# A small gather moved between two experts' products, with router logits by token, halved refills, nine taps on TensorE and x loaded first

## The reference, cut to what matters

```python
# first block, layer 0 (layer 1 has a recurrent mixer in place of conv_mixer)
u = x @ w_in                                     # 1024 -> 2560
a = a_val * sigmoid(a_gate)
a = causal_depthwise_conv(a, a_dw) + a_dw_b      # 31 taps, 512 channels
a = silu(layer_norm(a, a_ln_g, a_ln_b))
bb = b_b * causal_depthwise_conv(b_c * b_x, b_dw)
m = concatenate([a, bb]) @ w_out
x = layer_norm(ALPHA * x + m, ln1_g, ln1_b)
# route
logits = x @ w_router + b_router                 # 16 experts in 4 groups
probs = softmax(logits)                          # best group, then best 2 of its 4
# expert e on the tokens that chose it
y = (silu(xb @ w1[e]) * (xb @ w3[e])) @ w2[e]
x = layer_norm(ALPHA * x + f, ln2_g, ln2_b)
# second block, layer 0: forgetting attention, then conv_ffn; layer 1: dilated attention, then conv_ffn
h = rms_norm(x, mix_norm_g[layer])
log_f = log_sigmoid(h @ w_f + a_b_f)
```

## Time and profile before

| | us |
|---|---|
| timed, median of 3 | 1748.67 (1748.58 to 1749.48) |
| the profiled execution | 1751.06 |
| its span, first to last instruction | 1749.8 |
| granted clock of TensorE, mean over the span | 0.999 of full speed |

### The profile page before, as it was taken

One profiled execution on the slowest core, in us unless ns is written; L12 is line 12 of the kernel. 1 busy time (PEld: TensorE's weight loads), 2 busy tenths in 40 slices (PEclk: granted clock), 3 DMA queues, 4 the chain that ended last, 5 costly groups with the idle time before them and its releaser, 6 DMA issues.

```text
span 1749.8 us, 23960 instructions
## 1 busy us (share of the span) xinstructions
PE 1701.1 (97%) x9986; PEld 1114.9 (64%) x9986; DVE 791.5 (45%) x1520; ACT 625.8 (36%) x1203; POOL 131.2 (7%) x152
## 2 busy tenths in 40 slices
PE   9999999999899999999999989999999999999998
PEld 8974344433334984344343333887999899789997
DVE  6971111111103792111111012866888677868885
ACT  5541110000002670100010002666666564756665
POOL 0000000000001000000000001331111011301101
PEclk9999999999999999999999999999999999999999
DMA  9869999999999799999999999534555544435550
GB/s 380 331 241 401 422 429 428 428 427 428 426 425 419 291 377 393 424 428 430 428 427 427 426 424 420 190 124 144 172 191 183 202 161 154 141 137 171 191 193 24
DMA packets 56947, 544.88 MB, mean 311 GB/s; under 512 B 6400, under 2 KB 6400, under 8 KB 8832
## 3 DMA queue, kind: packets, MB, share of 16 engines
q1 hardware_dynamic: 56416, 542.14, 76.8%
q10 hardware_dynamic: 416, 1.13, 0.2%
HBM read 542.19 MB, written 1.05 MB: 310 GB/s over the span
## 4 chain that ended last, share of the span: by engine, by line
PE 75%; DMA 20%; DVE 4%; ACT 1%; POOL 0%; issue 0%; SPq 0%; ACTq 0%; DVEq 0%
PE PS L1313 22%; DMA ring<-in_w 20%; PE PS L440 13%; PE PS L442 13%; PE PS L441 13%; PE PS L1367 2%; PE PS L1295 2%; PE PS L1513 2%; PE PS L1021 1%; PE PS L2056 1%; PE PS L1329 1%; DVE wl L411 1%; PE PS L1381 1%; PE PS L1486 1%; DVE sm L650 0%; PE PS L2937 0%
## 5 line engine op out<-in xcount | busy, mean ns | idle before, releaser
L1313 PE MATMUL PS<-ring,F 128*64 128x512 f32 x1984 | 444.3, 595 | 26.2 <-DMA ring<-in_w 22.1
L411 DVE TENSOR_TENSOR wl<-ring,wh 128x512 fp32r<-128x512 f32 x496 | 359.3, 741 | 143.3 <-ACT wh L405 140.9
L405 ACT ACTIVATE wh<-ring 128x512 fp32r<-128x512 f32 x504 | 315.0, 630 | 267.8 <-PE PS L442 245.1
L1313 PEld LDWEIGHTS PS<-ring,F 128*64 128x64 f32 x1984 | 140.3, 137 | 306.9 <-issue 264.5
L440 PE MATMUL PS<-xh,wl 128*128 128x256 f32 x1128 | 325.2, 288 | 0.1
L441 PE MATMUL PS<-xl,wh 128*128 128x256 f32 x1128 | 319.2, 283 | 0.0
L442 PE MATMUL PS<-xh,wh 128*128 128x256 f32 x1128 | 319.2, 283 | 0.0
L440 PEld LDWEIGHTS PS<-xh,wl 128*128 128x128 f32 x1128 | 216.3, 192 | 2.7 <-DVE wl L411 0.9
L441 PEld LDWEIGHTS PS<-xl,wh 128*128 128x128 f32 x1128 | 216.4, 192 | 0.7
L442 PEld LDWEIGHTS PS<-xh,wh 128*128 128x128 f32 x1128 | 216.4, 192 | 0.0
L440 PE MATMUL PS<-wh,xl 128*128 128x512 f32 x320 | 129.7, 405 | 0.2 <-DVE F L2597 0.2
(11 more groups left out here) (451 smaller groups left out, 2056.5 us busy)
## 6 DMA issues: line engine op xcount, KB each, us to landing
ring<-in_w SPq DMA_DIRECT2D x98, 2048.0 KB, 25.6
ring<-in_w SPq DMA_DIRECT2D x68, 1024.0 KB, 12.2
ring<-in_ffn_up SPq DMA_DIRECT2D x44, 1024.0 KB, 4.9
early<-in_w SPq DMA_DIRECT2D x16, 2048.0 KB, 26.7
F<-in_w SPq DMA_DIRECT2D x15, 2048.0 KB, 26.5
F<-in_w SPq DMA_DIRECT2D x22, 1024.0 KB, 10.7
ring<-in_ffn_down SPq DMA_DIRECT2D x22, 1024.0 KB, 4.9
ZX<-in_w SPq DMA_DIRECT2D x7, 2048.0 KB, 26.8
```

The source lines that it names most:

```text
L405: act.e.activation(self.wh[:, p % NPIECE, :], self.piece_source(p), ACT.Copy).then_inc(*self.up("w_hi", p))
L411: dve.e.tensor_tensor(self.wl[:, p % NPIECE, :], self.piece_source(p), f32(self.wh[:, p % NPIECE, :]), ALU.subtract).then_inc(*self.up("w_ ...
L1313: t = pe.e.matmul(PS[64 * half:64 * half + 64, bank, :], lhs(k), weights[:, a:a + 512], start=(k == 0), stop=(k == 7))
```

## The change

Seven edits. (1) x is loaded in two halves ahead of all weights, and all of x is turned and split before the first weights are; `tensor_first_features` goes. (2) PE takes 9 taps instead of 11. ACT makes a first tap for each of the four channel groups (tap 9), DVE has the other 21; its table of steps is new, and the bias moves from the first tap to the closing sum. (3) Logits come by token (128 x 16), with the features as the loaded operand; the bias is a product with ones, and the turn of the logits and DVE's addition go. All four turns to tokens stand behind the logits, in the order 2, 3, 0, 1. (4) The next two features of the first pair are gathered between expert 0's and expert 1's chunk of a round. (5) Chunks 24, 25 and 26 of an expert layer are loaded in halves, the first as soon as the first half of the old chunk is used. (6) POOL's multiplication with the gain goes in halves of 512 columns, all but the first behind DVE's last low part; the shift of the second 128 tokens comes one slot later. (7) The spread of the row scales and what follows it in the forget gate come one slot later or share a slot.

```diff
-PE_TAPS = 11
+PE_TAPS = 9
...
+HALVED = {CHUNK[f"moe{layer}"] + 24 + i: layer for layer in range(2) for i in range(3)}
...
-    TURN_ORDER = (1, 2, 3, 0)
+    TURN_ORDER = (2, 3, 0, 1)
...
+            src = self.source(n)
+            if n in HALVED:
+                sp.wait_ge(self.at("expert_half", PREVIOUS[n]))
+                sp.e.dma_start(self.chunk(n)[:, 0:1024], src[:, 0:1024]).then_inc(self.s_last, 16)
+                sp.wait_ge(self.released(PREVIOUS[n]))
+                sp.e.dma_start(self.chunk(n)[:, 1024:2048], src[:, 1024:2048]).then_inc(self.ring_sems[SLOT[n]], 16)
+                continue
...
-        for j, pieces in enumerate((slice(0, 512), slice(512, 1024))):
+        for j in range(2):
             columns = slice(512 * j, 512 * j + 512)
             self.sp.e.dma_start(self.X[:, :, columns], x[:, :, columns]).then_inc(self.x_in[j][0], 16)
+        for j, pieces in enumerate((slice(0, 512), slice(512, 1024), slice(1024, 2048))):
             self.sp.e.dma_start(self.chunk(0)[:, pieces], self.source(0)[:, pieces]).then_inc(self.first_in[j][0], 16)
-        pieces = slice(1024, 2048)
-        self.sp.e.dma_start(self.chunk(0)[:, pieces], self.source(0)[:, pieces]).then_inc(self.first_in[2][0], 16)
...
-            for _ in self.tensor_features("ev", p + 4 * c, (6, 1, 2, 3, 4, 5, 0, 1, 4, 5)[c], c == 0):
-                for _ in range(0 if c < 3 or c > 8 else 1 if c == 8 else 2):
+            for _ in self.tensor_features("ev", p + 4 * c, (6, 1, 2, 3, 4, 5, 0, 1, 4, 5)[c]):
+                for _ in range(0 if c < 3 or c > 7 else 1 if c == 7 else 2):
...
-        high(0)
-        high(1)
-        self.scalar_split(0)
-        high(2)
-        self.scalar_split(1)
-        high(3)
-        for n in (2, 3):
+        for q in range(4):
+            high(q)
+        for n in range(4):
             self.scalar_split(n)
...
+                for ch in {(2, 0): (0, 1), (4, 0): (2, 3)}.get((c, j), ()):
+                    act.wait_ge(at("ev_dve", 1 + 2 * (ch // 2)), at("ev_pad"))
+                    act.e.activation(v["acc"][:, ch, :], v["aP"][:, ch, PE_TAPS:PE_TAPS + 256], ACT.Copy,
+                                     scale=v["aw"][:, ch, PE_TAPS:PE_TAPS + 1]).then_inc(*up("ev_first_tap", ch))
...
-        steps = {(1, 3): [(value, 0)], (2, 0): [(convolve, 2)], (2, 1): [(convolve, 1)], (2, 2): [(convolve, 2)],
-                 (2, 3): [(convolve, 1)], (3, 3): [(convolve, 3), (value, 1)], (5, 3): [(convolve, 2), (product, 0)],
-                 (6, 3): [(convolve_b, 0)], (7, 3): [(convolve, 2), (product, 1)], (8, 2): [(convolve_b, 1)],
-                 (8, 3): [(convolve, 2), (gate_b, 0)], (9, 0): [(convolve, 2)], (9, 2): [(convolve, 1)], (9, 3): [(gate_b, 1)]}
+        steps = {(1, 3): [(value, 0)], (2, 0): [(convolve, 1)], (2, 1): [(convolve, 2)], (2, 2): [(convolve, 2)],
+                 (2, 3): [(convolve, 2)], (3, 3): [(convolve, 2), (value, 1)], (5, 3): [(convolve, 2), (product, 0)],
+                 (6, 3): [(convolve_b, 0)], (7, 0): [(convolve, 3)], (7, 1): [(convolve, 3)], (7, 2): [(convolve, 3)],
+                 (7, 3): [(convolve, 1), (product, 1)], (8, 0): [(convolve, 2)], (8, 1): [(convolve, 2)],
+                 (8, 2): [(convolve_b, 1)], (8, 3): [(gate_b, 0)], (9, 0): [(convolve, 2)], (9, 1): [(convolve, 1)],
+                 (9, 2): [(convolve, 2)], (9, 3): [(gate_b, 1)]}
...
-                for step, n in steps.get((c, j), [(convolve, 4 if (c, j) in ((4, 1), (5, 1), (6, 1)) else 3)] if c > 2 else []):
+                for step, n in steps.get((c, j), [(convolve, 4)] if c > 2 else []):
...
-        return self.PS[64 * h:64 * h + 16, 2 * h, 0:128]
+        return self.PS[:, h, 0:16]
...
+        if k == 0:
+            pe.wait_ge(self.br_in, self.at("consts", "ones"))
+            pe.e.matmul(self.logits_of(h), self.ones[0:1, 0:128], self.brow[:, :], start=True, stop=False)
...
-        t = pe.e.matmul(self.logits_of(h), wr[:, k, :], self.RT[:, k, h * 128:h * 128 + 128], start=k == 0, stop=k == 7)
+        t = pe.e.matmul(self.logits_of(h), self.RT[:, k, h * 128:h * 128 + 128], wr[:, k, :], start=False, stop=k == 7)
...
-        self.tensor_to_tokens(layer, self.RT, ready, frees, order[:1])
-        for h in range(2):
-            r = slice(64 * h, 64 * h + 16)
-            pe.wait_ge(at("logits_t", layer, h))
-            t = pe.e.transpose(PS[:, 6 + h, 0:16], self.lgT[r, :], self.ident[r, r])
-        t.then_inc(*up("logits_turned", layer))
-        self.tensor_to_tokens(layer, self.RT, ready, frees, order[1:])
+        self.tensor_to_tokens(layer, self.RT, ready, frees, order)
...
+        for k in range(2):
+            self.tensor_first_gather(layer, k)
         for c in range(4):
-            for kk in range(2):
-                self.tensor_first_gather(layer, 2 * c + kk)
             for ex in range(2):
+                if ex and c < 3:
+                    for k in (2 * c + 2, 2 * c + 3):
+                        self.tensor_first_gather(layer, k)
...
+                    if kk == 0 and (c, ex) in ((0, 0), (0, 1), (1, 0)):
+                        t.then_inc(*self.up("expert_half", n))
...
-            if s in (-8, -7):
-                h = s + 8
-                dve.wait_ge(at("x_gain", h))
+            if s in (-8, -6):
+                h = (s + 8) // 2
+                dve.wait_ge(at("x_gain", h, 1))
...
-            pool.wait_ge((self.s_row, 32), self.half_normed("moe1", h, 0), self.half_normed("moe1", h, 1))
-            e.tensor_tensor(self.X[:, h, :], self.Z[:, h, :], self.last_rows()[:, 0, :], ALU.mult).then_inc(*up("x_gain", h))
+            for d in range(2):
+                columns = slice(512 * d, 512 * d + 512)
+                pool.wait_ge((self.s_row, 32), self.half_normed("moe1", h, d))
+                if (h, d) == (0, 1):
+                    pool.wait_ge(at("x_lo", "fg", 3))
+                e.tensor_tensor(self.X[:, h, columns], self.Z[:, h, columns], self.last_rows()[:, 0, columns],
+                                ALU.mult).then_inc(*up("x_gain", h, d))
```

More of the change, by code:

```diff
@@ L76 @@
     ("ev_ready", "ev_consts ev_pad"), ("norm_stats", "stats moments var_eps less_mean"),
-    ("norm_scale", "rstd shift"), ("route", "logits_t logits_less_max route chosen ranks_read"),
+    ("norm_scale", "rstd shift"), ("route", "logits_less_max route chosen ranks_read"),
     ("gating", "gating gate_slots counts_read overflow_flag"),
-    ("routed", "logits logits_turned ranked counted"),
+    ("routed", "logits ranked counted expert_half"),
     ("od_recur", "od_rate od_gating od_gated od_input od_state od_join"),
@@ L449, in tensor_busy @@
             self.pe.e.matmul(self.PS[:, bank, 0:256], self.ident[:, :], self.ones[:, :], start=True, stop=True)
-    def tensor_first_features(self, stage, p, out, xh, xl):
-        pe = self.pe
-        for k in range(8):
-            h, l = self.weight(p + k // 4)
-            a = slice(k % 4 * 128, k % 4 * 128 + 128)
-            pe.wait_ge(self.at("x_hi", stage, k // 2), self.low_made(p + k // 4))
-            pe.e.matmul(out, l[:, a], xh[:, k, :], start=k == 0, stop=False)
-            pe.e.matmul(out, h[:, a], xh[:, k, :], start=False, stop=False)
-        for k in range(8):
-            h, l = self.weight(p + k // 4)
-            a = slice(k % 4 * 128, k % 4 * 128 + 128)
-            pe.wait_ge(self.at("x_lo", stage, k // 2))
-            t = pe.e.matmul(out, h[:, a], xl[:, k, :], start=False, stop=k == 7)
-            if k % 4 == 3:
-                t.then_inc(*self.up("w_used", p + k // 4))
-                yield p + k // 4
     def first_chunk(self, stage):
@@ L531, in tensor_first_normed_chunk, with tensor_features @@
         low(3)
-    def tensor_features(self, stage, p, bank, first=False):
+    def tensor_features(self, stage, p, bank):
         pe, PS = self.pe, self.PS
@@ L537, in tensor_features @@
         for j in range(2):
-            if first and j == 0:
-                yield from self.tensor_first_features(stage, p, PS[:, bank, 0:256], xh, xl)
-                continue
             for k in range(8):
@@ L1127, in low @@
                                 ALU.subtract).then_inc(*up("x_lo", "ev", q))
-        low(0)
-        low(1)
-        self.vector_split(0)
-        low(2)
-        self.vector_split(1)
-        low(3)
-        for n in (2, 3):
+        for q in range(4):
+            low(q)
+        for n in range(4):
             self.vector_split(n)
@@ L1147, in even_vector @@
         p = PIECES["ew_in"]
-        taps = [(k, c) for half in range(2) for k in range(PE_TAPS, 31) for c in (2 * half, 2 * half + 1)]
+        taps = [(k, c) for half in range(2) for k in range(PE_TAPS + 1, 31) for c in (2 * half, 2 * half + 1)]
         def value(half):
@@ L1461, in moe_tensor_route @@
         order, ready = self.TURN_ORDER, (lambda h, k: self.route_feature(layer, h, k))
[L1462 to L1469 removed]
+        frees = [[at("logits_less_max", layer)], [], [], []]
+        self.tensor_to_tokens(layer, self.RT, ready, frees, order)
```

(11 more changed lines are left out.)

44 lines of the change are left out of this document (18 added, 26 removed).

## The result

The changed kernel takes 1755.76 us (median of six, 1752.48 to 1757.59) against 1748.83 for the kernel before on the same chip: 1.0037 times its time, 95% interval 1.0027 to 1.0047. It is 6.9 us slower; 4.2 us faster was forecast, and the range ended at 1748.4.

The account below looks back on a forecast made before the run. TensorE, busy 97%, was taken to limit the first stage and the weight stream to end each expert stage. Terms +0.5 − 3.2 + 0.4 − 1.75 = −4.05 us gave a median of 1744.6 us, range 1741.8 to 1748.4.

Parts of the forecast that it names:

- Input first: Start of the kernel: x's second half arrives at 7.37 us instead of 8.21, but first products end later; cost +0.5 us.
- Nine taps: First stage: eight diagonal products fewer on TensorE save 3.44 us, less 0.2 for a late low part; −3.2 us.
- R3: Rival, chance 0.10: DVE limits the first stage, its last sum 1.6 us later instead of 3.2 sooner; 1749.4 us.
- Logits by token: Both routes: dearer logits products and filler pushed behind the chosen mask cost +0.4 us a layer, bounds 0.15 and 0.6.
- R2: Rival, chance 0.14: late refills bind in the expert stages, +1.66 us a layer instead of +0.2; 1747.5 us.
- Gathers and halved refills: Expert stages: half a chunk reloaded 0.9 us earlier, later release seldom empties the queue; −0.2 us a layer.
- R4: Rival, chance 0.14: halves start each layer's stream 0.9 us earlier, filler costs nothing; −0.75 us a layer, 1742.7 us.
- Gain in halves: Final norm before the second block: DVE's subtractions end sooner, waits at line 520 go; −1.75 us, bounds −2.6 and −0.4.
- a wait below 1 us: Expected sign: TensorE's wait at the first features product after the forget logits stays below 1 us.
- R5: Rival, chance 0.12: GpSimd contention only moves to X's sum and the splits; −0.4 us instead of −1.75, 1746.0 us.
- Forget slots: Forget gate: the later spread, scan and cut have a slot or more of slack each; no cost.
- A shift of the first stage that does not arrive at the end of the expert stage: Named as outright refutation: time saved ahead of a route was claimed to come through as an earlier refill.

Follow-up runs that it names:

- e1: Kernel before with edit (3) alone, the router's logits by token with 16 streamed columns: 1756.76 us, 1.0041 times before.
- e6: Kernel before with edits (1) and (2) alone, x loaded first and nine taps on TensorE: 1746.61 us, ratio 0.9986.
- e7: Kernel before with edits (4) and (5) alone, gathers between the two experts' products and refills in halves: 1750.15 us, ratio 1.0004.
- e3: Kernel before with edits (6) and (7) alone, the gain in halves and the forget gate's slots shifted: 1750.73 us, ratio 1.0006.
- e8: Kernel before with edit (2) alone, nine taps on TensorE in place of eleven: 1746.13 us, ratio 0.9980.
- e5: e1 with each logits product streaming 128 columns in place of 16, only the first 16 results read: 1750.67 us, ratio 1.0008 to the kernel before.
- e9: The whole change with each logits product streaming 128 columns in place of 16: 1749.20 us, ratio 0.9998 to the kernel before.
- e11: Kernel before with edits (2) and (6) alone, nine taps and the second norm's gain in halves: 1746.30 us, ratio 0.9985.
- e4: Kernel before with edit (6) alone, the gain in halves without the shift of slots: 1749.88 us, ratio 1.0001.
- after: The whole change, all seven edits on the kernel before: 1755.76 us, 1.0037 times before; its profiled span is 1753.9 us.
- e13: e10 with every logits product loading 128 by 128 weights in place of 128 by 16: 1753.49 us, ratio 1.0026 to the kernel before.
- e10: Kernel before, logits by feature, six middle products of each eight streaming 16 columns in place of 128: 1749.17 us, ratio 1.0000.

## Why the prediction was wrong

The parts add up. The ratios of e1 (+0.41%), e6 (−0.14%), e7 (+0.04%) and e3 (+0.06%) sum to +0.37%, which is that of the whole, though each has an interval of about ±0.1%. By the steps of the prediction:

- **Input first, +0.5.** The second half of x was turned at 7.11 us (7.2 to 7.6 was said) and the first product came at 10.36 (10.4 to 10.8), both just ahead of their ranges. The step took the arrival as fixed; over four profiles it lies between 6.31 and 8.22 us, so that the size isn't resolved.
- **Nine taps, −3.2.** Right: the averaging product at 89.25 us for 92.01, with 89.1 to 89.6 forecast, and e8's median 3.1 us lower. VectorE's sums end at 88.75, 0.5 us ahead of it, and after it VectorE waits 0.64 for TensorE. R3 is out. The chain rows of the changed kernel:

```profile
87.08 1.67 DVE L1189 SCALAR_TENSOR_TENSOR F<-F,sm,PS 128x256 f32<-128x256 f32 x4
...
89.25 1.89 PE L1021 MATMUL PS<-F,mean 128*128 128x256 f32 x8
...
91.18 1.22 DVE L1197 TENSOR_TENSOR F<-F,PS 128x1024 f32<-128x1024 f32 x1 [0.64 <-PE PS L1021]
```

- **Logits by token, +0.4 a layer.** This is the step that failed. "28 instructions take 3.1" and the filler pushed behind the mask were right as far as they go: at full clock e5 shows 0.67 and 0.74, of which 0.3 are its wider products (24 in 2.94 us; at the pitch of 0.11 they would take 2.64). Two slips of the sum don't matter: 0.9 − 0.79 is 0.11 and not 0.15, and R2 has 0.5 for a route that the sum has at 0.4. But the step took every later duration in the route from a row at a clock of 1.0. At 0.5 the turns and the filler behind the logits take longer, and the filler's end, the very thing I had named as late next, moves with them. The missing term measured 3.1 us a route (e1 against e5), and 3.1 and 1.4 in the change's profile, whose second fall is the shorter (13.48 for 10.41, 12.06 for 10.63 in e9); the medians of the change and e9 differ by 6.6 us. The bounds 0.15 to 0.6 had no case in which the clock isn't 1.0, because the trace of before has no such stretch ahead of its end.
- **Gathers and halved refills, −0.2 a layer.** Measured +0.9 for two layers, the interval from −0.9 to +2.3. The halves were issued 0.86 apart, as said (130.85 and 131.71 us); the rate fell with them. The sign leans to R2's side, though the transfer engines stayed busy, which speaks for the smaller transfers rather than the late slot; the interval takes in the −0.4 forecast for two layers, and R4's −0.9 a layer is outside it.
- **Gain in halves, −1.75.** The waits at L520 went as said, but "a wait below 1 us" became 2.9 in three places. I priced 3.1 us for waiting and holding (the subtractions' end at 96.5, the split's at 101.5, with 1.9 of work between); e11's rows show the idle 1.47, +1.09 on the sum and +1.08 on the splits: 3.6 us against the 3.3 that the subtractions gave back. That is R5's mechanism, larger than R5 had it: 0, not −0.4. I also followed the chain only to the split: the second sum behind it came later, and with it the row scales, 0.4 us later than before (15.13 for 14.69).
- **Forget slots, nothing.** Right in the time (660.86 for 660.90), not in the slack of a slot that was its reason: e4 waits 1.5 us for the spread, and e3, with the slots shifted, 0.3 there and 1.4 for the keys.
- **"A shift of the first stage that does not arrive at the end of the expert stage"** was named as what would make it wrong outright. It does arrive (e8). What made it wrong was on no list. TensorE's waits for expert weights, said to stay near 22 us, came to 16.0, beside 9.1 of "issue" for 4.1.

With the clock's term left out the measured parts make −2.6 (e6) + 1.4 (e5) + 0.9 (e7) + 1.4 (e3) = 1.1 us: no change that could be told from none, as e9 shows.

## What to carry to other kernels

Before turning a small product around so that its large side is the loaded one, ask what TensorE streams in that stretch, and not only how busy it is: here the granted clock halved with 16 columns behind loads of 128 by 128 and not with 128, and everything behind it paid. Read the granted clock by windows early after any change; here a padding of useless columns won back 6 us. Where GpSimd's work beside VectorE is the suspect, test it by taking it away, since moving it moves the stall with it; and try edits of a bundle singly, as one of them was worth more alone than the bundle of seven.

## What the runs showed of the hardware

- TensorE's clock fell from 2.4 to 1.2 GHz while the engine counted as 98% busy (after; 94% in e13's second route, 6.14 of 6.50 us), with 16 columns streamed behind loads of 128 by 128 (after, e1, e13). In the routes it stayed at 2.4 with 128 columns (e5) and with loads of 128 by 16 (e10).
- It also fell around a stretch in which TensorE stood idle (e8: 4.78 us idle, 0.5 from 438.9 to 445.7 us), at no cost, since the transfers ran on.
- The second half of x, loaded first, was turned at 6.31, 7.11, 7.64 and 8.22 us in four kernels with the same start, and the first route moved with it (112.94, 113.83, 114.39 and 115.30 us).
- Beside GpSimd a VectorE split of 128 by 512 took 1.75 us for 0.68, a sum of 128 by 1024 took 2.30 for 1.21.
